# A chain of two hybrid layers and one modulated block: preparation of the mixers inside the input projection, attention values per head, a modulation with two stationary columns, and a scan state without an identity product

## The reference, cut to what matters

```python
h = rms_norm(x, norm1_g)
mq, mk, mv, mo, mi, mf, aq, ak, av = split(h @ w_in)      # 7 x 512 columns, and 16 of gates
mq, mk = silu(centred_depthwise_conv([mq, mk], conv_w))    # width 5
# mLSTM, 4 heads of 128, forward and backward, from sums of log gates and running maxima
y_m = rms_norm_per_head(h_fwd + h_bwd) * head_norm_g * sigmoid(mo)
# dilated attention, 8 heads of 64, rotary embedding on aq and ak
y_a = dilated_attention(rope(aq), rope(ak), av)
x = x + [y_m, y_a] @ w_out
x = x + relu(rms_norm(x, norm2_g) @ w_up)**2 @ w_down
```

```python
mod_x = split(silu(c) @ w_mod + b_mod, 6)      # shift, scale, gate, shift, scale, gate
mod_c = split(silu(c_ctx) @ w_mod + b_mod, 6)  # of which shift and scale of the first norm are used
```

```python
def step(s, inp):
    w, kk, a, k, v, r = inp
    sa = einsum('dbhij,dbhj->dbhi', s, kk)
    s = s * w - sa * (kk * a) + v * k
    return s, einsum('dbhij,dbhj->dbhi', s, r)
```

## Time and profile before

| what | value |
|---|---|
| median of three runs | 5869.04 us (5867.03 to 5873.03) |
| the profiled execution | 5869.24 us, span 5867.2 us |
| PE busy | 4744.5 us, 81% |
| DVE busy | 3118.3 us, 53% |
| ACT busy | 1591.1 us, 27% |
| POOL busy | 712.8 us, 12% |
| mean granted clock | 0.88 |

### The profile page before, as it was taken

One profiled execution on the slowest core, in us unless ns is written; L12 is line 12 of the kernel. 1 busy time (PEld: TensorE's weight loads), 2 busy tenths in 40 slices (PEclk: granted clock), 3 DMA queues, 4 the chain that ended last, 5 costly groups with the idle time before them and its releaser, 6 DMA issues. The chain is left out here.

```text
span 5867.2 us, 59517 instructions
## 1 busy us (share of the span) xinstructions
PE 4744.5 (81%) x21680; PEld 3458.3 (59%) x21680; DVE 3118.3 (53%) x6175; ACT 1591.1 (27%) x3130; POOL 712.8 (12%) x588
## 2 busy tenths in 40 slices
PE   6679897949799768478689999997867777777777
PEld 5546786826688657256578888885756333333333
DVE  3453322273322022775376666663233888888886
ACT  2222431232333021241155554542221111111111
POOL 0000110000001000000000000000000444444443
PEclk9866898965899679698899999998988899999999
DMA  3000322200232331002300000001222999999998
GB/s 107 29 1 29 108 90 63 76 0 1 80 100 79 140 116 39 1 1 87 123 9 11 11 17 14 11 3 49 91 72 77 421 419 411 415 412 410 415 411 353
DMA packets 146752, 777.84 MB, mean 133 GB/s; under 512 B 19732, under 2 KB 26132, under 8 KB 78232
## 3 DMA queue, kind: packets, MB, share of 16 engines
q0 software_dynamic: 73728, 536.90, 22.3%
q1 hardware_dynamic: 72728, 237.07, 12.0%
HBM read 753.99 MB, written 19.92 MB: 132 GB/s over the span
## 5 line engine op out<-in xcount | busy, mean ns | idle before, releaser
L2280 PE MATMUL psum<-rows,diag 128*128 128x512 f32 x2048 | 1002.9, 647 | 313.1 <-ACT diag L2259 308.4
L2280 PEld LDWEIGHTS psum<-rows,diag 128*128 128x128 f32 x2048 | 412.0, 206 | 886.2 <-issue 886.2
L2170 POOL DMA_INDIRECT rows<-in_peer_uv,sel_idx x512 | 624.0, 1219 | 2293.2 <-DVE sel_idx L2118 1618.4
L337 DVE TENSOR_TENSOR w_split_lo<-w_raw,w_split_hi 128x1024 fp32r<-128x1024 f32 (+1 forms) x316 | 382.4, 1221 | 725.7 <-ACT w_split_hi L329 717.3
L2185 DVE SCALAR_TENSOR_TENSOR uh<-rows,h_rows 128x1024 f32<-128x1024 f32 x512 | 627.7, 1226 | 179.6 <-DMA rows<-in_peer_uv,sel_idx 151.6
L329 ACT CAST w_split_hi<-w_raw 128x1024 fp32r<-128x1024 f32 (+1 forms) x316 | 320.9, 1028 | 852.8 <-PE psum L284 552.5
L2252 ACT ACTIVATE g<-g 128x4 f32<-128x4 f32 x128 | 26.3, 205 | 1074.8 <-DVE g L2196 1074.8
L1449 PE MATMUL psum<-X_wide,wAT_wide 128*128 128x128 f32 x1920 | 262.2, 280 | 1.2 <-DVE X_wide L1783 1.2
L1449 PEld LDWEIGHTS psum<-X_wide,wAT_wide 128*128 128x128 f32 x1920 | 234.8, 192 | 34.0 <-issue 29.5
L1783 DVE COPY_PREDICATED X_wide<-rwc_level,psum 128x512 f32<-128x512 uint32 x192 | 137.8, 718 | 204.8 <-PE psum L1460 204.2
L529 POOL TENSOR_TENSOR uT_lo<-relu_squares,uT_hi 128x512 fp32r<-128x512 f32 x64 | 82.9, 1296 | 1235.8 <-ACT uT_hi L505 1235.8
(11 more groups left out here) (444 smaller groups left out, 9506.8 us busy)
## 6 DMA issues: line engine op xcount, KB each, us to landing
w_raw<-in_w_in SPq DMA_DIRECT2D x120, 512.0 KB
w_raw<-in_w_up SPq DMA_DIRECT2D x64, 512.0 KB
w_raw<-in_w_down SPq DMA_DIRECT2D x64, 512.0 KB
wbuf_mod<-in_w_mod SPq DMA_DIRECT2D x12, 2048.0 KB
w_raw<-in_w_out SPq DMA_DIRECT2D x24, 512.0 KB
w_raw<-in_peer_wq SPq DMA_DIRECT2D x16, 512.0 KB
rows<-in_peer_uv,sel_idx POOLq DMA_INDIRECT x512
w_raw<-in_w_branch_a SPq DMA_DIRECT2D x8, 512.0 KB
```

What stands on the lines that cost most here:

```text
L337: nc.vector.tensor_tensor(ring.lo[:, q % SPLIT_RING, :, 0:w], raw[:, q % raw_ring, :, 0:w], ring.hi[:, q % SPLIT_RING, :, 0:w].bitcast(F32 ...
L2170: nc.gpsimd.indirect_dma_start(out=rows[:, n % RB, :], out_offset=None, in_=I["peer_uv"], in_offset=bass.IndirectOffsetOnAxis(ap=sel[:, t, ...
L2280: last = nc.tensor.matmul(psum[:, 2 * (t % 2) + half, :], diag[:, n % (2 * BATCH), :], rows[:, n % RB, D + half * NB:D + (half + 1) * NB], ...
```

## The change

- The mLSTM's preparation moves into the input projection. gemm_phase takes a `side` object, whose programs for ACT and DVE are called behind each group of a block. Tables CONV_AT and SILU_AT give the (block, group) behind which each convolution and silu stands. The order of blocks becomes query, key, gates, attention queries, attention keys, mLSTM values, mo, attention values. qkpad is overwritten in place by silu; conv and the gate sums live in space of av and y.
- Rope's matmuls become groups of the projection (class Plain: one float32 product, not three), between those of the two blocks behind the attention keys, and DVE does the three passes when it empties them.
- The attention phase has no rope. DVE scales the probabilities before they are turned; values are made once per head, av stationary (64 columns) and 512 columns of turned probabilities moving, and come out turned. transpose_phase is gone: its mLSTM half is turned inside the attention phase, at units 0 to 3, and the high and low halves are written there.
- Modulation: the eight column blocks become `pair_groups`: csil (2 columns) is stationary, 512 columns of weights move, DVE copies two rows out; 32 small matmuls with a 2 x 2 identity then turn the rows to columns, and DVE adds the bias. The weight buffer has four slots instead of two.
- rwkv: the identity matmul is gone. ACT, in step 1, copies the old state scaled into wP; DVE makes state = sum x scale + wP in step 2, in its program between the solve's merge and its transpose (which moves behind it, function `turn`).

```diff
+class MixerPreparation:
+    CONV_AT = {(1, 0): 0, (1, 1): 1, (1, 2): 2, (1, 3): 3, (3, 3): 4, (4, 0): 5, (4, 2): 6, (4, 3): 7}
+    SILU_AT = {(1, 1): 0, (1, 2): 1, (1, 3): 2, (2, 0): 3, (4, 0): 4, (4, 1): 5, (4, 3): 6, (5, 0): 7}
...
+    def vector(self, dve, chain, b, g):
+        nc = self.nc
+        if (b, g) in self.CONV_AT:
+            self.convolve(dve, chain, self.CONV_AT[b, g])
+        if b == 3 and g in (1, 2):
+            self.sums(dve, chain, g - 1)
+        if b == 7 and g >= 1:
+            self.scale_gate(dve, g - 1)
+        if (b, g) == (7, 3):
+            self.scale_gate(dve, 3)
```

```diff
+            def both(w):
+                g = groups(w)
+                r = [(P, S, Plain([(T["rot"][:], aqk[:, first + j, :])], (source, j)), rope(first + j), "v")
+                     for j in range(4)]
+                return [g[0], r[0], g[1], r[1], g[2], r[2], r[3], g[3]]
...
-        gemm_phase(nc, psum, blocks, raw_ring=2)
-        normed.close()
...
+        side = MixerPreparation(nc, T, qkpad, v_ext, mo, gates, av, y)
+        gemm_phase(nc, psum, blocks, raw_ring=2, side=side)
...
+        attention_phase(nc, T, aqk, av, y, yT)
-    transpose_phase(nc, psum, ident, y, yT)
```

In the attention phase (PE's order, and DVE's):

```diff
-                scores(0)
-                for u in range(UNITS + 1):
-                    if u + 1 < UNITS:
-                        scores(u + 1)
-                    if u < UNITS:
-                        turn(u)
-                    if u >= 1:
-                        values(u - 1)
+                for v in range(UNITS + 3):
+                    if v < UNITS:
+                        scores(v)
+                    if v < MC:
+                        turn_y(v)
+                    if 2 <= v < UNITS + 2:
+                        turn(v - 2)
+                    if v >= 3 and (v - 3) % ST == ST - 1:
+                        values((v - 3) // ST)
...
+                    for k in range(ST):
+                        last = nc.tensor.matmul(psum[lo:lo + 64, 4 + pair % 2, :], av[:, k, h * A_DIM:(h + 1) * A_DIM],
+                                                pT[:, h % 2, k, :], start=(k == 0), stop=(k == ST - 1))
...
+                def scale(u):
+                    dve.wait_ge(probs_ready, u + 1)
+                    chain.after(nc.vector.reciprocal(st[:, 2, u:u + 1], st[:, 1, u:u + 1]))
+                    nc.vector.tensor_scalar(pr[:, u % 3, :], pr[:, u % 3, :], st[:, 2, u:u + 1], None, ALU.mult
+                                            ).then_inc(probs_scaled, 1)
```

Modulation and rwkv:

```diff
+        def pair_groups(q, half):
+            def groups(w):
+                dst = mod_rows[:, q, half * NB:(half + 1) * NB]
+                return [(2, NB, [(csil[:, c, :], w[:, c, :]) for c in range(DC)],
+                         lambda ch, acc: nc.vector.tensor_copy(dst, acc), "v")]
...
-    with nc.sbuf_tensor("wbuf_mod", [P, 2, DC * NB], F32) as wbuf:
+    with nc.sbuf_tensor("wbuf_mod", [P, 4, DC * NB], F32) as wbuf:
...
-                        if n:
-                            nc.tensor.matmul(S_, ident[:], wS[:], start=True, stop=False)
-                        else:
+                        if n == 0:
                             pe.wait_ge(bt_copied, 3 * u + 3)
                             pe.wait_ge(kt_copied, 3 * u + 3)
-                        nc.tensor.matmul(S_, flat(wkt[:, u % 2, c]), v, start=(n == 0), stop=False)
+                        nc.tensor.matmul(S_, flat(wkt[:, u % 2, c]), v, start=True, stop=False)
...
+                    if 0 < n < NCH - 1:
+                        act.wait_ge(pl_ready, u + 1)
+                        act.wait_ge(s_copied, 11 * u + n)
+                        nc.scalar.activation(wP[:], wS[:], ACT.Copy, scale=pl[:, u % 3, c:c + 1]
+                                             ).then_inc(s_decayed, 1)
...
+            def state(n, u):
+
+                c = orders[u % 2][n]
+                dve.wait_ge(s_ready, 11 * u + n + 1)
+                scale = pl[:, u % 3, c:c + 1]
+                if n:
+                    dve.wait_ge(s_decayed, 10 * u + n)
+                    nc.vector.scalar_tensor_tensor(wS[:], psum[:, 5, 0:P], scale, wP[:], ALU.mult, ALU.add
+                                                   ).then_inc(s_copied, 1)
...
                     if build is not None:
                         solve(k, build)
+                    if scanned is not None and k % 3 == 2 and k < SLOTS_ - 1:
+                        state(k // 3, scanned)
+                    if build is not None:
+                        turn(k, build)
                         if 3 <= k < 12:
                             fill(k, build)
```

More of the change, by code:

```diff
@@ L289, in _, with each @@
                     last.then_inc(sum_ready, 1)
-            def each(eng, which, split, chain):
+            def each(eng, which, split, chain, beside=None):
                 n = 0
@@ L317, in each @@
                             evac(chain, psum[0:rows, bank, 0:cols]).then_inc(emptied[e], 1)
+                        if beside is not None:
+                            beside(eng, chain, b, i - first_of_block[b])
             @block.scalar
@@ L339, in split @@
                                             ).then_inc(lo_ready, 1)
-                each(dve, "v", split, Chain(dve, vec_step))
+                each(dve, "v", split, Chain(dve, vec_step), side.vector if side else None)
             @block.gpsimd
             def _(pool):
+                if side is not None:
+                    side.gpsimd(pool)
                 if tail is not None:
@@ L633, in _ @@
                 dve.wait_ge(cols_copied, 1)
-                dve.wait_ge(gate_opened, 1)
-                for t in range(ST):
-                    chain.after(nc.vector.tensor_tensor(mo[:, t, :], mo[:, t, :], hng[:], ALU.mult))
                 def span(d, j):
@@ L1015, in modulation_phases, with _ @@
             for half in range(2):
-                g = row_groups(m // 3, half) if m in (2, 5) else column_groups(m, half)
+                g = row_groups(m // 3, half) if m in (2, 5) else pair_groups(PAIRS.index(m), half)
                 blocks.append((I["w_mod"][2 * m + half], g))
         plain_gemm_phase(nc, psum, wbuf, blocks)
-        with Phase(nc, ["vec_step"]) as (block, vec_step):
+        with Phase(nc, ["columns_ready", "vec_step"]) as (block, columns_ready, vec_step):
+            @block.tensor
+            def _(pe):
+                for q in range(len(PAIRS)):
+                    for c in range(DC):
+                        at = 2 * (q * DC + c)
+                        last = nc.tensor.matmul(psum[:, 0, at:at + 2], mod_rows[:, q, c * P:(c + 1) * P],
+                                                T["ident"][0:2, 0:2], start=True, stop=True)
+                last.then_inc(columns_ready, 1)
             @block.vector
@@ L2449, in second_block_program @@
         R["rows"] = sb("y_rows", [L_CH, XCH * P])
[L2450 removed]
+        for n in ("wS", "wP", "wW", "wN"):
             R[n] = sb(n, [P, P])
```

388 lines of the change are left out of this document (214 added, 174 removed).

## The result

The changed kernel takes 5638.31 us (median of 4, 5634.52 to 5644.80) against 5871.03 for the kernel before on the same chip (5867.03 to 5873.97): ratio 0.9605, 95% interval 0.9589 to 0.9622. It is 233 us faster. The forecast was 5609, 260 us faster; 5638 lies inside its range of 5550 to 5680, 29 us above the forecast; 2 of the 29 are the kernel before, whose median is 5871 here and was 5869 when the forecast was made. The profiled execution took 5638.48 us.

A forecast was written before the change was run, and what follows sets the result against it. Bounds: PE in projection and rwkv, DVE and ACT before mLSTM scores, PE at low clock in attention and modulation. 2 x (10 - 43 - 70.5) = -207, -43, -10: -260 from 5869.24, so 5609; range 5550 to 5680.

The forecast's parts named there:

- the wait that the prediction named: rwkv, slot 2: PE will wait some 0.6 us for the state, because DVE is busy with its queue.
- the two other slots that the prediction named: rwkv: late state costs about 0.8 to 1.5 us at slot 26 in every other iteration, 0.2 to 0.6 at slot 32.
- Projection and mLSTM: Input projection +10 us a layer; gap before the first mLSTM score -43 a layer; the 84 us behind are kept.
- The rope products: Input projection: 8 added matmuls on PE, 8 x 0.854 = 6.8 us.
- the growth of the waits for low halves: Input projection: PE's waits for DVE's low halves of weights grow by +2 us (bounds 0 and 10.5).
- rival of a slowed projection: Input projection: convolutions or silu waits delay the next weights' halves; +15 us a layer beyond +10, 5640; chance 0.15.
- Attention, the failed step: Attention loop: new loop taken at 2.4 GHz with DVE the bound; -70 us a layer.
- The rule weighed there: Attention: full clock does not engage for transposes, so the loop would start cold; some 10 us a layer more.
- Modulation: Modulation stage: all twelve blocks with weights moving, PE the bound at 7.1 us a block; -43 us (-30 to -48).
- Its rival (0.50 for two stationary columns): Modulation stays at 1.2 GHz, 14.2 us a block; +10 in place of -43, 5662; chance 0.12.
- The attention's second rival: Attention stays at or falls back to 1.2 GHz; -24 us a layer instead of -70, 5699; chance 0.07.
- rwkv: rwkv stage: identity matmul removal saves 35.5 us of PE, late states cost 25; -10 us (-35 to +10).

The follow-up runs named there:

- scan_alone: The kernel before with the scan part alone (identity product out, state on DVE): 5860.33 against 5868.21 us, ratio 0.9996 (0.9986 to 1.0006).

## The attention: what held the clock

The changed kernel's first attention stretch in windows of 4 us:

```profile
330.00:334.00 4.00, 4.00 (x12) 2.17 (x12) 3.07 (x6) 1.84 (x5) 0.00 (x0) 0.50 0.00 0
...
342.00:346.00 4.00, 4.00 (x8) 1.54 (x9) 2.82 (x7) 1.88 (x4) 0.00 (x0) 0.50 0.00 0
346.00:350.00 4.00, 4.00 (x8) 0.91 (x6) 0.00 (x0) 0.69 (x3) 0.00 (x0) 0.74 0.00 0
...
374.00:378.00 4.00, 3.21 (x12) 1.21 (x10) 2.61 (x6) 1.77 (x4) 0.00 (x0) 1.00 0.00 0
378.00:382.00 4.00, 2.12 (x6) 1.22 (x6) 3.59 (x8) 2.11 (x6) 0.00 (x0) 0.60 0.01 4
382.00:386.00 4.00, 4.00 (x9) 1.37 (x8) 1.94 (x4) 1.75 (x4) 0.00 (x0) 0.55 0.00 0
```

The clock is 0.50 for the first 25 us, in which PE has only scores and transposes, though PE is busy 24.11 of the 25 us from 321; it rises within the first block of values (started at 344.90). It falls again at 378 and again at 406, for some 7 us each, each time behind a stretch in which PE has gaps, and once more at 430, for the end of the loop. The second layer repeats this to 0.1 us. The timeline shows the gap at the first fall, and beside it a normal unit and the place of a values block:

```profile
364.47 0.68 DVE L936 SCALAR_TENSOR_TENSOR sc<-psum,amask_sb 128x512 f32<-128x512 f32 x1
...
366.38 0.68 DVE L936 SCALAR_TENSOR_TENSOR sc<-psum,amask_sb 128x512 f32<-128x512 f32 x1
...
369.16 3.65 PE L915 MATMUL psum<-pT,av 128*64 128x512 f32 x8
...
373.90 0.69 DVE L936 SCALAR_TENSOR_TENSOR sc<-psum,amask_sb 128x512 f32<-128x512 f32 x1 [3.60 <-PE psum L895]
...
377.22 0.69 DVE L950 TENSOR_TENSOR hT_lo<-psum,hT_hi 128x512 fp32r<-128x512 f32 x1 [1.32 <-ACT hT_hi L986]
377.83 0.68 DVE L936 SCALAR_TENSOR_TENSOR sc<-psum,amask_sb 128x512 f32<-128x512 f32 x1
...
379.88 1.12 PE L903 MATMUL psum<-ident_sb,pr 128*128 128x128 f32 x4 [2.21 <-DVE pr L944]
```

A unit is 1.91 us of DVE (366.38 - 364.47), one behind a values block 5.60 (373.90 - 368.29). Four units are then 3 x 1.91 + 5.60 = 11.3 us where the forecast had 4 x 2.15 + 2.85 = 11.45. So while the clock is up four units take what was forecast, but by luck: the unit is 0.24 shorter than priced, and the block holds the next mask back by 3.69 (5.60 - 1.91), not by 2.85. At 377.22 DVE stands 1.32 us for ACT's high half of an output pair. The next mask is late by it, and with it the scaled probabilities: PE stands 2.21 us for them, and its transposes at 379.88 take 1.12 where those at 1.00 take 0.66. The clock is gone. Six kernels test this, each an edit of the changed kernel.

**old_loop**: the attention loop and the transposes of before (its diff is that of the attention phase, backwards), with rope staying in the projection.

> The joined kernel with the attention loop and the transpose phase of before (values per unit, 64 columns moving, output scaled at the end), rope staying in the projection. Theory: the loop's form is what holds the clock at 0.50; the stretch from first score to the output projection's first matmul is then 166.7 us as before, against 127.5 in the changed kernel: +39 a layer, 5716 (5710 to 5724). Rival: the old loop was cold because it followed a gap behind the rope products, and rises to 1.00 here: under 5690.

Measured: 5724.77, ratio 0.9752 (0.9735 to 0.9768), 86 over the changed kernel and just over the expected range. The stretch that the theory names is 166.3 us in the trace (323.96 to 490.3), as expected. The traced execution is the longest of the four (5739), for a reason in the rwkv stage (section on the scan). Its loop:

```profile
328.00:474.00 146.00, 144.68 (x444) 95.64 (x444) 53.80 (x126) 40.66 (x96) 0.00 (x0) 0.50 0.00 1
```

The form of the loop, not its place behind the rope products, holds 0.50 for 146 us, with PE busy 144.68. The rival falls.

**values_spread**: the values of a head cut into its four units.

```diff
-                    for k in range(ST):
-                        last = nc.tensor.matmul(psum[lo:lo + 64, 4 + pair % 2, :], av[:, k, h * A_DIM:(h + 1) * A_DIM],
-                                                pT[:, h % 2, k, :], start=(k == 0), stop=(k == ST - 1))
-                    last.then_inc(values_ready, 1)
+                    q = slice(i * P, (i + 1) * P)
...
+                    for k in range(ST):
+                        last = nc.tensor.matmul(psum[lo:lo + 64, 4 + pair % 2, q], av[:, k, h * A_DIM:(h + 1) * A_DIM],
+                                                pT[:, h % 2, k, q], start=(k == 0), stop=(k == ST - 1))
...
-                    if v >= 3 and (v - 3) % ST == ST - 1:
-                        values((v - 3) // ST)
+                    if v >= 3:
+                        values(v - 3)
```

> The joined kernel with each head's values made unit by unit: the same products cut to 128 moving columns, four behind each turn, instead of four of 512 behind every fourth. Theory A: the clock rises only behind the long block of 512-column products with 128 rows, so this loop stays at 0.50 for all of its units, at 1.7 + 0.85 + 1.7 us of PE each: 4.3 x 32 = 138 instead of 104 to the last mask, +34 a layer, 5706. Theory B: any loop without 64-column records rises; then no block stands ahead of the scores, units run at 1.91 us: 104 becomes some 75, -29 a layer, 5580.

Measured: 5598.91, ratio 0.954 (0.9525 to 0.9556): 39 us under the changed kernel.

```profile
326.00:334.00 8.00, 8.00 (x22) 4.33 (x22) 6.30 (x13) 3.06 (x7) 0.00 (x0) 0.50 0.00 0
342.00:366.00 24.00, 24.00 (x128) 14.04 (x126) 17.49 (x38) 11.60 (x28) 0.00 (x0) 1.00 0.00 1
```

Theory A falls at once: the clock rises as soon as this loop has values at all (the first are at 334.80, the window 338 to 342 is at 1.00), without any long block, and it stays up to the end. Theory B has the direction, but not the size: a unit is 2.66 us, not 1.91. The timeline shows why:

```profile
360.71 1.12 PE L895 MATMUL psum<-aqk 64*128 64x512 f32 x2
...
361.76 0.66 PE L903 MATMUL psum<-ident_sb,pr 128*128 128x128 f32 x4
...
362.35 1.09 PE L917 MATMUL psum<-pT,av 128*64 128x128 f32 x8
...
363.36 1.12 PE L895 MATMUL psum<-aqk 64*128 64x512 f32 x2
```

From 360.71 to 363.36 PE has no gap: 1.05 for scores, 0.59 for the turn, 1.01 for the values, each 0.15 to 0.2 more than its records' pitch gives, the excess lying where one kind of product follows another. PE is the bound there, and 2.66 is under the 2.83 of (3 x 1.91 + 5.60)/4. And PE has no gap in it: the clock stays at 1.00 to 422. Of the 39 us, 21 remain against out_late below, which keeps the blocks and has no falls between them.

**out_late**: DVE makes the low half of an output pair one unit later.

```diff
-                    if v >= 8 and v % 8 == 7 and v >= 15:
-                        out_part((v - 15) // 8)
+                    if v >= 16 and v % 8 == 0 and v < UNITS:
+                        out_part((v - 16) // 8)
+                out_part(PAIRS - 2)
                 out_part(PAIRS - 1)
```

> The joined kernel with DVE's low half of an output pair one unit later, so that DVE doesn't wait for ACT's high half. Theory: that wait (the mask intervals of 3.93 us in place of 1.91) empties PE and lets the clock fall twice a layer; without it the two falls go, and with them about 2.0 - 0.7 + 1.4 + 0.9 = 3.6 us each: -7 a layer, 5624 (5620 to 5630). Rival: the light load of the three short units is what lets the clock fall; the falls stay and only the wait goes, 1.3 us each: 5633.

Measured: 5619.52, ratio 0.9578 (0.9562 to 0.9594): 19 under the changed kernel, 9 a layer.

```profile
350.00:418.00 68.00, 61.18 (x191) 22.86 (x190) 45.97 (x98) 31.81 (x74) 0.00 (x0) 1.00 0.00 1
```

```profile
376.59 0.68 DVE L950 TENSOR_TENSOR hT_lo<-psum,hT_hi 128x512 fp32r<-128x512 f32 x1
377.19 0.68 DVE L936 SCALAR_TENSOR_TENSOR sc<-psum,amask_sb 128x512 f32<-128x512 f32 x1
```

The same instruction now has no wait before it, and both falls are gone: 1.00 over 68 us. The short units between blocks are as light as before, so the rival (the light load alone) falls. From 321.89 to 449.37 the changed kernel has 127.5 us, this one 117.3 (321.01 to 438.31). The gain is 10, not the expected 7 for a layer. The two falls gave 3.7 and 3.8 as expected (3.6 each); I had left out that the third pair's wait and the slow turns at the end go too, 2.4 behind the last mask.

**warm_start**: eight products on PE at the end of the mLSTM phase, with no use but the clock.

```diff
                     values(n)
+                for _ in range(8):
+                    nc.tensor.matmul(psum[:, 0, :], ident[:], qk[:, 0, :], start=True, stop=True)
```

> The joined kernel with eight products of 128 rows x 512 columns put on PE at the end of the mLSTM phase, where it idles 7 us; their result is not used. Theory: the attention's first units cost 3.37 us instead of 1.91 to 2.6 because they start at 0.50 and nothing in them lifts the clock; started at 1.00 they save 6 to 9 us a layer: 5623 (5618 to 5630). Rival: the gap at the barrier or the first units' waits lower the clock again before it counts: within 4 us of 5638.

Measured: 5641.99, ratio 0.9615 (0.9599 to 0.9631): no gain. The theory falls in an instructive way.

```profile
330.00:334.00 4.00, 2.53 (x12) 1.37 (x13) 2.88 (x6) 1.92 (x6) 0.00 (x0) 1.00 0.00 0
...
338.00:342.00 4.00, 3.76 (x9) 1.69 (x8) 3.86 (x9) 1.74 (x5) 0.00 (x0) 0.50 0.01 2
```

```profile
327.75 0.69 DVE L962 TENSOR_TENSOR hT_lo<-psum,hT_hi 128x512 fp32r<-128x512 f32 x1 [1.35 <-ACT hT_hi L995]
328.35 0.68 DVE L938 SCALAR_TENSOR_TENSOR sc<-psum,amask_sb 128x512 f32<-128x512 f32 x1
```

The clock was 1.00 for the first four units, and they still took 3.37 us each (328.35 to the next mask at 331.72), as at 0.50: DVE waits 1.35 in the first and 0.76 in each of the next three for ACT's high half of the turned mLSTM half, the same kind of wait as that of the output pairs. In the changed kernel the same waits stand in the trace, but PE at 0.50 is busy through the same units, so either could be taken for the limit. With PE that idle, the clock fell all the same behind the fourth unit. The first seven mask intervals together are 2.0 us shorter than in the changed kernel, and the intervals behind them, where the later falls come at other places in this run, 4.6 longer; the ends give back 1.8: that is how the start's gain came to nothing.

**late_warm**: out_late, warm_start, and DVE's low half of the turned chunks one unit later as well:

```diff
-                    if v < MC:
-                        dve.wait_ge(y_rounded, v + 1)
-                        nc.vector.tensor_tensor(yT.lo[:, v, :], psum[:, 8 - MC + v, :],
-                                                yT.hi[:, v, :].bitcast(F32), ALU.subtract).then_inc(y_low, 1)
+                    if 1 <= v <= MC:
+                        dve.wait_ge(y_rounded, v)
+                        nc.vector.tensor_tensor(yT.lo[:, v - 1, :], psum[:, 7 - MC + v, :],
+                                                yT.hi[:, v - 1, :].bitcast(F32), ALU.subtract).then_inc(y_low, 1)
```

> The kernel of out_late with DVE's low halves of the turned mLSTM half one unit later too, and the eight products of warm_start. In warm_start the first four units took 3.37 us at a clock of 1.00, as at 0.50. Theory: two limits of the same size lie on them, the chain mask, exp, high half, low half, mask through DVE and ACT, and PE's 3.4 us at 0.50; with both gone units 0 to 3 run at 2.0 to 2.7 us, the load is high enough to keep 1.00, and units 4 to 6 run at 1.91: -8 to -9 a layer against 5619.5, 5602 (5596 to 5608). Rival: the clock falls in the first units whatever their pace, as in warm_start at unit 4: above 5613.

Measured: 5606.04, ratio 0.9548 (0.9532 to 0.9563), 13 under out_late against the 17 of the theory. The traced execution is the longest of the four (5623), again for the reason in the rwkv stage; its attention, from the first score to the output projection, is 110.8 us a layer against 117.3, which is the 13.

```profile
322.00:326.00 4.00, 4.00 (x19) 2.04 (x19) 3.62 (x7) 2.31 (x7) 0.00 (x0) 1.00 0.00 0
...
330.00:334.00 4.00, 2.43 (x10) 1.40 (x10) 3.90 (x10) 3.06 (x7) 0.00 (x0) 0.92 0.01 2
```

Two limits of one size did lie on the first units: with both gone they take 2.51, DVE alone. But behind the last turned chunk, before the first values block, PE has the least to do (2.43 of 4), and the clock falls once: the first values block (from 337.34) begins at half of it. Theory and rival each have half of it. Scores and transposes alone did keep a clock of 1.00 here; in the changed kernel they did not raise it.

**halves_late**: values for two units at once, 256 columns moving, and both low halves late.

> Values made for two units at once, 256 columns moving, and both low halves one unit later. In values_spread PE was busy in every window, 2.66 us a unit, of which scores and turns are 1.28 by the pitch of their records and the values' eight short records the rest. Theory: the same columns in half as many records cost less, 1.0 us a unit, and the block of 2 us is short enough for DVE's head start: 2.2 to 2.3 a unit, -11 to -14 a layer against 5598.9, 5573 (5568 to 5582). Rival: DVE's wait behind each block comes back, or the clock falls in the lighter loop: 5590 or above.

Measured: 5614.35, ratio 0.957 (0.9554 to 0.9586), 15 slower than values_spread, though it has the late low halves that values_spread lacks: the rival holds.

```profile
350.00:422.00 72.00, 65.67 (x249) 30.12 (x247) 46.82 (x100) 32.82 (x77) 0.00 (x0) 1.00 0.00 1
```

```profile
383.19 0.68 DVE L939 SCALAR_TENSOR_TENSOR sc<-psum,amask_sb 128x512 f32<-128x512 f32 x1
...
387.08 0.69 DVE L939 SCALAR_TENSOR_TENSOR sc<-psum,amask_sb 128x512 f32<-128x512 f32 x1 [1.90 <-PE psum L895]
```

The clock is 1.00, but DVE waits 1.90 behind every block (1.30 where a low half fills a part of it), and PE is idle 6.3 of 72 us. Masks go 1.92 and 3.90 apart in turn, 2.91 a unit against 2.66. I read it so that two score buffers give DVE too little head start even for a block of 2 us; no kernel with a third buffer was run. In the spread loop the wait is 0.65 a unit, on an engine that is not the bound.

## The scan

In the changed kernel two iterations take 137.54 us where they took 138.0 (period of one kind of matmul in both traces). The removed product is 20 x 0.222 = 4.4 us; 4.0 of them came back. Slot 2 of an iteration:

```profile
3196.54 0.69 DVE L1872 STREAM_TRANSPOSE X_wide<-Y_wide 128x512 f32<-128x512 f32 x1
...
3197.16 0.30 DVE L1855 TENSOR_SCALAR wS<-psum,pl 128x128 f32<-128x128 f32 x1
...
3197.51 0.49 PE L1594 MATMUL psum<-wS,wq_wide 128*128 128x128 f32 x2 [0.31 <-DVE wS L1855]
```

PE's sum was ready at 3194.4 (L1616, 3193.98 + 0.39); DVE had its solve to do first, and wrote the state at 3197.46. That is the wait that the prediction named. Over the two iterations from here (3197.6 to 3335) PE's longest waits are these (total us, count, longest us):

```profile
PE psum L1566 <- ACT wkt_wide L1730: 1.9, 2, 1.0
PE psum L1594 <- DVE wS L1852: 1.1, 2, 1.0
```

The second row is the state again: 0.97 at slot 26 and 0.15 at slot 32, each in every other iteration, the two other slots that the prediction named. With 0.31 at slot 2 in both, the late states are 1.7 of the 4.0 us. Another 1.0 is in the first row, a wait for ACT's copy of wkt_wide, which was 0.9 over two iterations before; its growth was in no term. The remaining 1.3 shows in no wait.

**scan_first_act**: this first state of an iteration, a scaled copy without an old state, goes back to ACT.

```diff
+                elif n == 0:
+                    act.wait_ge(pl_ready, u + 1)
+                    act.wait_ge(s_ready, 11 * u + 1)
+                    nc.scalar.activation(wS[:], psum[:, 5, 0:P], ACT.Copy, scale=pl[:, u % 3, c:c + 1]
+                                         ).then_inc(s_copied, 1)
...
-                    if scanned is not None and k % 3 == 2 and k < SLOTS_ - 1:
+                    if scanned is not None and k % 3 == 2 and 3 <= k < SLOTS_ - 1:
                         state(k // 3, scanned)
```

> The joined kernel with the scan's first state of each iteration, which has no old state to add, made by ACT again. Theory: PE's wait of 0.42 us in slot 2 (0.59 us between the records where 0.17 was), once in each of 16 iterations, goes: 137.54 becomes 136.7 us for two iterations, -7 in all, 5631. Rival: the wait moves to the next slot, since what PE does there stands behind the same queue of DVE: the period stays within 0.2 us of 137.54.

```profile
3195.81 0.37 ACT L1749 ACTIVATE wS<-psum,pl 128x128 f32<-128x128 f32 x1 [0.41 <-PE psum L1616]
...
3198.38 0.39 PE L1594 MATMUL psum<-wS,wq_wide 128*128 128x128 f32 x2
```

The state is there 2.2 us before it is read, the wait is gone, and the period is 136.4 us: 1.2 less for two iterations, 9 for the stage, more than the 7 expected; the waits at slots 26 and 32 stay. The total is 5636.73 (ratio 0.9606, 0.9589 to 0.9623), 2 us under the changed kernel's median. Its four executions are two at 5628 and 5631 and two at 5642 and 5647, so the stage shows the gain and the median can't.

The traces show what can part them. In 8 of the 10 traces with the changed scan, and in all 4 with the old one, the clock is 1.00 in the last iteration. In late_warm and old_loop it fell to 0.50 within 1.1 us of that iteration's first product with the state, and stayed there. The last iteration in late_warm, and the same piece in out_late:

```profile
3773.00:3822.00 49.00, 45.04 (x151) 32.37 (x152) 4.19 (x11) 8.84 (x32) 0.00 (x0) 0.51 0.00 1
```

```profile
3786.00:3818.00 32.00, 26.51 (x152) 18.80 (x152) 4.61 (x12) 8.84 (x32) 0.00 (x0) 1.00 0.00 1
```

The same work takes 17 us more, which is the distance of scan_alone's two groups and of late_warm's traced execution from its others. The last iteration has no solve beside the scan, so PE has less to do in it than in those before. Whether the form of the changed scan makes the fall possible was not tested; that none of the 40 and more executions of the kernel before is over 5875 speaks for it.

## The version that beats both

**best_joined** is values_spread with both low halves late, the eight products, and the first state on ACT.

> values_spread (5598.9) with both low halves one unit later, the eight products at the end of the mLSTM phase, and the first state of an iteration on ACT. If the gains add: the output parts' units 3.93 + 1.91 + 3.05 become three of 2.66, -0.9 twice a layer; the first five units 3.37 x 3 + 4.83 become 2.5 to 2.7 each, -4 a layer; the scan -9 once, as its stage showed: 5598.9 - 3.6 - 8 - 9 = 5578 (5572 to 5586). Rival: the scan's 9 us do not reach the end, as the 2 us between medians in scan_first_act suggest: 5587.

Measured: 5569.39 us (5566.38 to 5570.93), ratio 0.9486 (0.9473 to 0.9499): 303 us under the kernel before and 69 under the changed one.

```profile
318.00:420.00 102.00, 92.77 (x477) 53.69 (x475) 70.93 (x152) 47.74 (x107) 0.00 (x0) 0.98 0.04 13
```

The clock is 0.98 over the whole phase. From the first attention score to the output projection's first matmul are 97.3 us (324.02 to 421.35), against 127.5 in the changed kernel. From unit 4 on every unit is 2.66: also at the output parts, where values_spread had 3.93, 1.91 and 3.05. It is 9 us better than the 5578 of the sum. The attention has 6 of them: the phase is 9.0 us a layer shorter than in values_spread (97.3 against 106.3) where 5.8 was summed, 1.3 more in the first five units, 1.0 in the first score, which now runs at the full clock, and 0.8 behind the last mask. The scan gave its 9. The other 3 us were not traced to a place.

## Why the prediction was right or wrong

- **Gain and order of size**: right. The largest terms were found by their stages: the wait for DVE and ACT ahead of the mLSTM's scores, a saturated PE at 0.50 in attention, PE at 0.50 in the modulation.
- **Projection and mLSTM**: -29.1 where -33 was forecast. The end of the phase gave what was forecast, 46.7 us from the last product to the first score before and 4.2 now. The rope products were priced right: from 165.57, where the first of them starts, to the second ordinary record behind it (166.66) are 1.09 us, 0.23 of them the ordinary record's, so 0.86 a product against 0.854. So was the growth of the waits for low halves: behind the start of the phase they were 3.5 us before and are 5.5 now (19.1 in all, 13.6 of it the start), the +2 taken. Two things were in no term. One is what a wait does to the clock. The wait came where the forecast had it, behind the gates, and by its path: a convolution on DVE (99.06) puts the gates' low halves to 102.61, SP issues the next load at 103.19 where it was 99.43, and from there ACT waits for the DMA, DVE for ACT and PE for DVE. One row of ACT, one of DVE, one of PE and a window right behind:

```profile
113.45 1.04 ACT L351 CAST w_split_hi<-w_raw 128x1024 fp32r<-128x1024 f32 x1 [4.12 <-DMA w_raw<-in_w_in]
114.53 1.22 DVE L359 TENSOR_TENSOR w_split_lo<-w_raw,w_split_hi 128x1024 fp32r<-128x1024 f32 x1 [3.94 <-ACT w_split_hi L351]
...
115.81 0.67 PE L304 MATMUL psum<-hT_hi,w_split_hi 128*128 128x512 f32 x1 [3.32 <-DVE w_split_lo L359]
```

```profile
116.00:118.00 2.00, 2.00 (x6) 1.52 (x6) 1.45 (x2) 1.05 (x2) 0.00 (x0) 0.50 0.38 94
```

  PE waits 3.3 us there in one piece; before it had two waits of 1.1 and 1.3 there and kept its clock. Now the clock falls with the gap, and the next nine records are 0.43 apart instead of 0.23: 1.8 us. The other is that the ordinary products are farther apart all through the new projection: 0.227 us before (eleven from 216.81 to 219.31), 0.229 up to the rope products and 0.233 behind them (nine from 231.69 to 233.79). Over 660 records that is 2.7 us. Every kernel here with the new projection shows it, and the feed-forward behind it doesn't (0.227); its cause stays open. The rival of a slowed projection (+15 a layer by waits) did not come. That the measured 5638 stands beside that rival's 5640 is chance.
- **Attention, the failed step**: -57.8 a layer where -70.5 was forecast, 25 of the 29 us. The step is "The new loop is made of just these two kinds, so I take 2.4 GHz". It took a clock that dense stretches had raised as the clock of a loop with waits (the 1.00 from 357 to 360 is that of the rope products themselves; in the kernel before it was 0.50 again from 364, before the loop began). The loop starts at 0.50 and keeps it while it has only scores and transposes, and it loses 1.00 whenever an ordering wait between DVE and ACT opens a gap. Four units at 1.00 came out within 1%, 11.3 for 11.45, by two errors that cancel (1.91 for 2.15 a unit, 3.69 for 2.85 a block). I had seen the outputs' steps only as DVE time (2 us in all), and not named who waits for whom in them. out_late gives 10 of the 12.7 us back; the cold start is the rest, the first seven mask intervals being 27.2 us where the forecast's terms give 24.5 (4 x 3.80 + 2 x 2.15 + 5.0).
- **The rule weighed there**: the start was cold, and the first values block lifted it. The prediction priced this case at some 10 us a layer; by the intervals above it cost 2.7. That the stage is off by 12.7 all the same is the falls' doing, which no case had. The Trainium skill (TensorE: Matmul & The Clock Gate, Part 4) says that the full clock does not engage for transposes. Here both are seen: 32 transposes without a gap raised it, transposes between scores of 64 rows did not. I let one row outweigh the rule for a loop that was not like the row.
- **Modulation**: -44.1 against -43. Two terms were off and partly cancelled: the first block landed 7.4 us behind its issue, not 10.5; the turning back, whose products took 11.5 at a clock of 0.63, added 12, not 10. The four buffers were worth nothing measurable. Its rival (0.50 for two stationary columns) fell: the first block's timeline has its records 0.85 apart at first and 0.43 from the sixth on. By the forecast's own terms that rival was dearer than stated: 10.5 + 160 + 10 less today's 152.6 are +28, not +10, so 5680 and not 5662. (The attention's second rival comes to 5702 likewise, not 5699.)
- **rwkv**: -7.2 against -10, by the mechanism forecast and at its three slots. The late states cost less than forecast there, 0.31, 0.97 and 0.15 us for 0.6, 0.8 to 1.5 and 0.2 to 0.6, 14 in all for the 25 taken. With a wait for ACT, 8 in all, and some 10 that show in no wait, 32 of the 35.5 would come back at the pace of the steady iterations, a gain of 3.7; the other 3.5 came in the scan's last two iterations, which no term treated apart. That the sum came near is in part luck.

## What to carry to other kernels

A forecast of a PE-bound loop at the higher clock needs its gaps as well as its work: follow every short wait between the other engines in it, since 1.3 us of waiting three times a layer cost 10 us here. A block of products put ahead of the next unit's input holds the engine that feeds on it; cutting the same products evenly over the units won 39 us (21 of them beyond what the gaps had cost), though at 1.00 PE's time for them rose from 0.90 to 1.01 us a unit. Where two limits of the same size lie on a stretch, taking one away shows nothing: test them together before the theory is dropped.

## What the runs showed of the hardware

Blocks of products with two stationary columns and 512 moving raised the clock from 0.50 with the sixth record of the first block and kept it at 1.00 behind it, in 7.03 us a block, as with 128 stationary columns (7.10). The loop with 64 moving columns kept PE busy 144.68 of 146 us at 0.50; in values_spread, where the same products have their operands exchanged, the clock was 1.00 within 4 us of the first of them. In values_spread a change from one kind of product to the next goes with 0.15 to 0.2 us more of PE, and 8 records of 128 columns take 1.01 us where their pitch of 0.109 gives 0.87.
